# Hyena's transforms folded over mirrored tokens, and its filters' transforms over even and odd times

## The chip, the core and the metric

The kernel runs on one core of a Trainium2 chip. The metric is the device time of one execution in microseconds (us), median of several runs. TensorE is PE in the rows (PEld its weight loads), VectorE DVE, ScalarE ACT, GpSimd POOL, SyncE SP; SP issues the DMAs. All engines run their own instruction streams in the order written and meet only at semaphores.

## The reference, cut to what matters

Two blocks of layers follow each other. The first has two layers on 512 tokens (x) and 256 context tokens (ctx). Of its mixers (attention of 8 heads, a Fourier mix, a Hyena mix) the change touches the Hyena mix and the filters that it convolves with:

```
def hyena_filters(L, w1, b1, freq, w2, b2, w3):
    ...
    h = jnp.sin(freq * (h @ w2 + b2))
    h = (h @ w3).astype(f32)
    ...
    h = h * jnp.tile(decay, (1, 2))
    h_fwd, h_bwd = h[:, :HYENA_W], h[:, HYENA_W:]
    k = jnp.concatenate([h_fwd, jnp.zeros((1, HYENA_W), f32), h_bwd[:0:-1]], axis=0)
    return k / jnp.sum(jnp.abs(k), axis=0, keepdims=True)

def hyena_mix(u, conv_w, conv_b, w1, b1, freq, w2, b2, w3, d_bias):
    u = short_conv(u, conv_w, conv_b)
    x0, x1, v = jnp.split(u, 3, axis=-1)
    z = (x1 * v).astype(jnp.float32)
    k = hyena_filters(L, w1, b1, freq, w2, b2, w3)
    zf = jnp.fft.rfft(z, n=2 * L, axis=1)
    kf = jnp.fft.rfft(k, n=2 * L, axis=0)
    y = jnp.fft.irfft(zf * kf[None], n=2 * L, axis=1)[:, :L] + d_bias.astype(jnp.float32) * z
    return (x0.astype(jnp.float32) * y).astype(u.dtype)
```

HYENA_W is 256 channels. Layer 0 mixes x (L = 512) and ctx (L = 256), layer 1 only x. So there are three filters: two for 512 times (0 and 1), one for 256 (2).

## The kernel before

Stages follow each other with a barrier between them. In the stages that matter here every piece of work is a "thread" that yields due times (plain numbers), and `run_braided` writes each engine's program by merging the threads in order of those times. The numbers only set the order; an engine waits at a semaphore wherever it has to.

**The opening** (`opening`) loads and turns the tokens (`EnterThread`), multiplies the condition vector with a layer's modulation weights (`ModulationThread`, L3068 on PE), and makes the three filters (`FilterThread`). A filter is two small layers with sines, then L3283 on PE, scaled by the decay on DVE (L3335) and formed into sum and difference `pm` (L3337, L3338), the sum of magnitudes (L3289), its reciprocal on DVE, and the transform L3300: per block f of 128 frequencies, 2 parts (cosine, sine) times `nt` tiles of 128 times, each an fp32 product of 128x256 with the table `tk`. DVE scales the result into `kf` (L3350). PSUM bank 7 serves the even blocks of all three filters; the odd ones have a bank per filter. SP stores the filters to memory, and the next stage starts after these stores.

**The mixers** (`mixers`, once a layer) put the attention in units of two 128-token blocks, in pitch W. In a unit u PE does scores(u) (L1688), the turning of the first half of the last unit's probabilities (L1703), values of the unit before that (L1715), the turning of the other half (L1703), and then a fill: a piece of other work. scores(u+1) waits for ACT's second exponential of unit u, and that one waits for the second turning, whose buffer it writes. The fills are the heads' projections (L1570 to L1582) and the Hyena work (`HyenaThread`): `fill(u)` is unit u's place. Layer 0 has 24 units and ctx's Hyena work too, layer 1 has 16 units.

The Hyena thread of one sequence: DVE convolves and multiplies to z (`col(4 + b)`, b = 0, 1, two groups of 128 channels) early in the stage; at fill(0) (ctx: fill(10)) PE turns z (L1844) and ACT keeps it as `zt` (L1878); per block f PE transforms it with the table `ta` (L1857), a bank for both parts, and DVE multiplies with the filter into `yf` (L1915 to L1920); per b PE transforms back with the same table (L1867) and DVE adds d*z and multiplies with x0 (L1926, L1929). In layer 0 the four blocks f of x are at fill(1), (2), (4), (5), the two inverses at fill(7), (8); ctx has both f at fill(11) and both b at fill(13). In layer 1 two blocks f are at fill(1), two at fill(3), the inverses at fill(5) and fill(7). On DVE, unit u's maximum (L1774), reciprocal (L1780) and scaling (L1782) stand at due times 2.6 and 3.6 after the unit's start.

An fp32 matmul of the program is two PE records in the trace; a turning is one.

## Time and profile before

| | |
|---|---|
| runs (us) | 3737.94, 3743.83, 3743.93; median 3743.83 |
| profiled execution | span 3744.0 us; no other time of that execution is given |
| PE busy | 3505.1 us (94%), 17782 records |
| PEld / DVE / ACT / POOL busy | 76% / 53% / 36% / 4% |
| opening, 0 to 135 us | PE busy 106.2, DVE 65.3, ACT 34.3 |
| mixers of layer 0, 268 to 560 us | PE busy 270.0, DVE 147.6, ACT 100.5 |
| mixers of layer 1, 1310 to 1475 us | PE busy 157.0, DVE 83.9, ACT 55.1 |

A matmul's record lasts longer than the distance to the next one, since matmuls are pipelined; what a group of them costs is read from the start of the first to the start of what follows. An idle time in brackets is that of the engine just before the row, with what ended it.

### The profile page before, as it was taken

The numbers are of one execution on the slowest core, as the hardware profiler recorded it, in microseconds if no ns is written. First come the engines' busy times: TensorE is split into PE (matmuls) and PEld (weight loads), VectorE is DVE, ScalarE is ACT, GpSimd is POOL, SyncE is SP. The second block draws the span as 40 slices with busy tenths as digits, with TensorE's granted clock in tenths as the row PEclk, the third lists the DMA queues.
The fourth block names the chain that finished last, engine by engine and source line by source line (L and its number), as shares of the span: only waits on it lengthen the run. The fifth ranks groups of instructions, "written<-read, shape, count | busy, mean of one in ns | idle before, by whom it ended". The sixth has DMA issues, their size and how long they took to land.

```text
span 3744.0 us, 42762 instructions
## 1 busy us (share of the span) xinstructions
PE 3505.1 (94%) x17782; PEld 2844.8 (76%) x17782; DVE 1971.7 (53%) x2697; ACT 1352.1 (36%) x1896; POOL 144.0 (4%) x108
## 2 busy tenths in 40 slices
PE   7899988899999999889998997999889999979998
PEld 2684557788888755688887887888778888778887
DVE  5566446577655454466556665333445455553333
ACT  3322334422323333353345556222433333362223
POOL 0000000000000000000000004000400000040001
PEclk9999999999999999999998998999999999989998
DMA  5442003345444230145532221323233323213231
GB/s 177 129 153 72 12 1 109 111 149 162 152 157 130 79 107 1 46 140 185 192 117 68 68 68 57 98 94 99 59 81 72 87 68 90 67 57 102 90 99 48
DMA packets 366624, 360.65 MB, mean 96 GB/s; under 512 B 65071, under 2 KB 312030, under 8 KB 365023
## 3 DMA queue, kind: packets, MB, share of 16 engines
q1 hardware_dynamic: 366211, 357.84, 31.2%
q8 instruction: 141, 2.31, 0.3%
q14 instruction: 52, 0.43, 0.0%
q10 hardware_dynamic: 220, 0.07, 0.0%
HBM read 350.02 MB, written 4.72 MB: 95 GB/s over the span
## 4 chain that ended last, share of the span: by engine, by line
PE 47%; DVE 5%; ACT 4%; POOL 1%; issue 1%; DMA 0%; SPq 0%; POOLq 0%; DVEq 0%; ACTq 0%
PE ps L403 41%; PE ps L2530 1%; DVE r_st L2424 1%; ACT second_w_hi L490 1%; DVE second_w_lo L549 1%; ACT second_scr L685 1%; PE ps L2551 1%; PE ps L2553 1%; POOL sums L467 1%; PE ps L2303 1%; POOL sq L464 1%; PE ps L2540 1%; DVE x_res L870 0%; DVE second_scr L868 0%; DVE second_scr L696 0%
## 5 line engine op out<-in xcount | busy, mean ns | idle before, releaser
L403 PE MATMUL ps<-second_h_hi,second_w_hi 128*128 128x512 f32 (+1 forms) x2216 | 831.4, 375 | 51.6 <-DVE second_h_lo L896 18.1
L403 PE MATMUL ps<-second_h_hi,second_w_lo 128*128 128x512 f32 (+1 forms) x2216 | 811.8, 366 | 0.0
L403 PE MATMUL ps<-second_h_lo,second_w_hi 128*128 128x512 f32 (+1 forms) x2216 | 811.8, 366 | 0.0
L549 DVE TENSOR_TENSOR second_w_lo<-ring,second_w_hi 128x2048 fp32r<-128x2048 f32 (+2 forms) x176 | 390.5, 2219 | 480.6 <-ACT second_w_hi L490 480.6
L403 PEld LDWEIGHTS ps<-second_h_hi,second_w_hi 128*128 128x128 f32 x2216 | 430.2, 194 | 120.2 <-issue 29.4
L403 PEld LDWEIGHTS ps<-second_h_hi,second_w_lo 128*128 128x128 f32 x2216 | 429.0, 194 | 65.4
L403 PEld LDWEIGHTS ps<-second_h_lo,second_w_hi 128*128 128x128 f32 x2216 | 430.3, 194 | 63.4 <-issue 1.9
L490 ACT ACTIVATE second_w_hi<-ring 128x2048 fp32r<-128x2048 f32 (+2 forms) x176 | 311.4, 1769 | 309.1 <-PE ps L403 301.0
L403 PE MATMUL ps<-h_mix_hi,w_hi 128*128 128x512 f32 (+3 forms) x776 | 272.2, 351 | 24.0 <-DVE h_mix_lo L712 16.5
L403 PE MATMUL ps<-h_mix_lo,w_hi 128*128 128x512 f32 (+3 forms) x776 | 268.7, 346 | 0.0
L403 PE MATMUL ps<-h_mix_hi,w_lo 128*128 128x512 f32 (+3 forms) x776 | 268.0, 345 | 0.0
L403 PEld LDWEIGHTS ps<-h_mix_hi,w_hi 128*128 128x128 f32 (+1 forms) x776 | 148.8, 192 | 45.6 <-issue 11.1
L403 PE MATMUL ps<-hid_hi,w_hi 128*128 128x256 f32 (+1 forms) x512 | 173.5, 339 | 0.0
L403 PE MATMUL ps<-hid_lo,w_hi 128*128 128x256 f32 (+1 forms) x512 | 172.3, 337 | 0.0
L403 PE MATMUL ps<-hid_hi,w_lo 128*128 128x256 f32 (+1 forms) x512 | 172.1, 336 | 0.0
L1072 DVE SCALAR_TENSOR_TENSOR side_a<-side_w,cond,side_a 128x512 f32<-128x512 f32 x224 | 157.2, 746 | 21.7 <-DMA side_w<-in_w_mod 16.8
L490 ACT ACTIVATE w_hi<-ring 128x2048 fp32r<-128x2048 f32 x50 | 95.3, 1905 | 187.4 <-PE ps L403 180.4
L403 PEld LDWEIGHTS ps<-h_mix_lo,w_hi 128*128 128x128 f32 (+1 forms) x776 | 148.7, 192 | 18.1 <-issue 0.8
L403 PEld LDWEIGHTS ps<-h_mix_hi,w_lo 128*128 128x128 f32 (+1 forms) x776 | 148.3, 191 | 18.0
L549 DVE TENSOR_TENSOR w_lo<-ring,w_hi 128x2048 fp32r<-128x2048 f32 x50 | 114.6, 2292 | 80.5 <-ACT w_hi L490 80.5
L403 PE MATMUL ps<-second_hid_hi,second_w_hi 128*128 128x512 f32 (+1 forms) x424 | 152.0, 358 | 0.0
L403 PE MATMUL ps<-second_hid_lo,second_w_hi 128*128 128x512 f32 (+1 forms) x424 | 151.0, 356 | 0.0
(402 smaller groups left out, 5763.9 us busy)
## 6 DMA issues: line engine op xcount, KB each, us to landing
ring<-in_w_mlp SPq DMA_DIRECT2D x64, 1024.0 KB, 5.4
side_w<-in_ada_w SPq DMA_DIRECT2D x96, 512.0 KB, 4.8
ring<-in_ffn_w_in SPq DMA_DIRECT2D x44, 1024.0 KB, 5.1
side_w<-in_w_mod SPq DMA_DIRECT2D x80, 512.0 KB, 3.9
ring<-in_attn_w_in SPq DMA_DIRECT2D x48, 512.0 KB, 5.3
ring<-in_hgrn_w_in SPq DMA_DIRECT2D x32, 512.0 KB, 4.9
ring<-in_ffn_w_out SPq DMA_DIRECT2D x16, 1024.0 KB, 5.0
ring<-in_w_in SPq DMA_DIRECT2D x14, 1024.0 KB, 5.5
```

The source lines that it names most:

```text
L403: mm = pe.matmul(acc, lhsT, rhs, start=k == 0 and wp == ap, stop=k == j.kt - 1 and wp == 1)
L464: pool.tensor_tensor(dst[:, 1, :], y, x, ALU.mult).then_inc(*S["sums_product"].one)
L467: pool.tensor_tensor(acc[:, parts, :], acc[:, parts, :], dst[:, parts, :], ALU.add).then_inc(*S["sums_added"].one)
L490: act.activation(unit.place(unit.slot[0]), unit.place(M.ring[:, u % RING, :]), ACT.Copy).then_inc(*S.w_hi.one)
L549: dve.tensor_tensor(unit.place(unit.slot[1]), unit.place(M.ring[:, u % RING, :]), unit.place(unit.slot[0]), ALU.subtract).then_inc(*S.w_lo ...
L685: f = act.activation(scr[:, k, :], scr[:, k, :], ACT.Identity, scale=self.scale(ks.start + k, a), bias=self.bias(ks.start + k, a))
L1072: p = dve.scalar_tensor_tensor(a, src, col, a, ALU.mult, ALU.add)
L2303: mm = pe.matmul(M.ps[:, 5, c], B.st[:, m, :], B.qs[:, c], start=False, stop=m == self.N_CHUNKS - 1, skip_group_check=True)
L2424: o = dve.scalar_tensor_tensor(B.st[:, m + 1, :], B.st[:, m, :], B.eb[:, m * CHUNK + CHUNK - 1:m * CHUNK + CHUNK], add, ALU.mult, ALU.add)
L2530: mm = pe.matmul(self.y_ps[:, i * P:(i + 1) * P], values, p_t(i)[:, k, :], start=m == 0, stop=m == len(tiles) - 1)
L2540: tr = pe.transpose(self.t_ps[:, k * P:(k + 1) * P], M.f[:, i % 2, k * P:(k + 1) * P], M.ident[:, :])
L2551: pe.matmul(self.s_ps[:, 0:LX], every4(qk[:, 0, :], u), qk[:, 1, :], start=True, stop=True)
```

## The change

**Hyena transforms.** DVE forms, just ahead of fill(0) (fill(10) for ctx), sum and difference of z and mirrored z into the new tile `uv`, and PE turns `uv` in the place of z. A block f then needs one half of the turned tiles for each part: nt/2 products in the place of nt, with the table `ta` of half the size. The inverse makes two half results (for sum and difference) of length/2 columns each, with a table `ti`, and DVE unfolds them: two operations add d*z, two add or subtract the other half, each on half the columns. The two tables of a sequence are two DMAs in the place of one, with the same bytes together; `uv` lies where the Fourier tables and later `yf` lie. **Filters.** The times are sorted into even and odd ones (decay and embedding too). A pair of blocks of frequencies needs one transform of the even and one of the odd times, each nt/2 products a part, and their sum and difference are the two blocks. DVE scales each half into `mag` and then forms sum and difference on 128x512 elements. The table `tk` has half the bytes: 1 MB in the place of 2 MB for 512 times.

```
-        self.ta = sb("mx_ta", [P, self.nt, 2, length], 44)
+        self.half = length // 2
+        self.ta = sb("mx_ta", [P, self.nt // 2, 2, length], 44)
+        self.ti = sb("mx_ti", [P, self.nt, 2, self.half], 52)
+        self.uv = sb("mx_uv", [P, 2, length], 64)
...
-        sp.dma_start(self.ta[:, :, :, :], X.io[f"hy_ta_{self.length}"]).then_inc(*S.landing("hyena_ta_landed").one)
+        landed = S.landing("hyena_tables_landed")
+        sp.dma_start(self.ta[:, :, :, :], X.io[f"hy_ta_{self.length}"]).then_inc(*landed.one)
+        sp.dma_start(self.ti[:, :, :, :], X.io[f"hy_ti_{self.length}"]).then_inc(*landed.one)
...
-                tr = pe.transpose(M.ps[:, bank, t * P:(t + 1) * P], self.col(4 + b)[:, t * P:(t + 1) * P],
-                                  M.ident[:, :])
+                tr = pe.transpose(M.ps[:, bank, t * P:(t + 1) * P], self.uv[:, b, t * P:(t + 1) * P], M.ident[:, :])
...
             for c in range(2):
-                for t in range(nt):
+                folded = (c + self.odd(f)) % 2 * (nt // 2)
+                for t in range(nt // 2):
                     mm = pe.matmul(M.ps[:, bank, c * HY:(c + 1) * HY], self.ta[:, t, c, f * P:(f + 1) * P],
-                                   self.zt[:, t, :], start=t == 0, stop=t == nt - 1)
+                                   self.zt[:, folded + t, :], start=t == 0, stop=t == nt // 2 - 1)
...
-            X.banks.claim(pe, bank, (S["hyena_part"], self.z0 + b + 1))
+            X.banks.claim(pe, bank, (S["hyena_part"], 2 * (self.z0 + b) + 2))
             pe.wait_ge(S["hyena_mixed"].sem, S["hyena_mixed"].at(self.f0 + nt))
-            for f in range(nt):
-                for c in range(2):
-                    mm = pe.matmul(M.ps[:, bank, 0:length], self.yf[:, f, c, b * P:(b + 1) * P], self.ta[:, f, c, :],
-                                   start=f == 0 and c == 0, stop=f == nt - 1 and c == 1)
+            for part in range(2):
+                for f in range(nt):
+                    c = (part + self.odd(f)) % 2
+                    mm = pe.matmul(M.ps[:, bank, part * self.half:(part + 1) * self.half],
+                                   self.yf[:, f, c, b * P:(b + 1) * P], self.ti[:, f, c, :], start=f == 0, stop=f == nt - 1)
...
-                dve.tensor_tensor(self.col(b), self.col(b - 2), self.col(b), ALU.mult).then_inc(*S["hyena_z"].one)
+                dve.tensor_tensor(self.col(b), self.col(b - 2), self.col(b), ALU.mult).then_inc(*S["hyena_product"].one)
+        yield self.t_z - 1.5
+        dve.wait_ge(S["hyena_product"].sem, S["hyena_product"].at(self.z0 + 2))
+        dve.wait_ge(S["fourier_acc"].sem, S["fourier_acc"].at(2 if X.last else 4))
+        if self.before:
+            dve.wait_ge(S["hyena_acc"].sem, S["hyena_acc"].at(self.z0))
+        h, n = self.half, self.length
+        for b in range(2):
+            z = self.col(4 + b)
+            dve.tensor_tensor(self.uv[:, b, 0:h], z[:, 0:h], z[:, n - 1:h - 1:-1], ALU.add)
+            dve.tensor_tensor(self.uv[:, b, h:n], z[:, 0:h], z[:, n - 1:h - 1:-1], ALU.subtract)\
+                .then_inc(*S["hyena_z"].one)
...
-            z, x0 = self.col(4 + b), self.col(b)
-            part = S["hyena_part"]
-            dve.scalar_tensor_tensor(z, z, M.col("hy_d", X.l, b), M.ps[:, 6 + b, 0:self.length], ALU.mult, ALU.add)\
-                .then_inc(*part.one)
-            dve.wait_ge(part.sem, part.at(self.z0 + b + 1))
+            z, x0, h, n = self.col(4 + b), self.col(b), self.half, self.length
+            even, odd = M.ps[:, 6 + b, 0:h], M.ps[:, 6 + b, h:n]
+            part, d = S["hyena_part"], M.col("hy_d", X.l, b)
+            up, down = z[:, 0:h], z[:, n - 1:h - 1:-1]
+            dve.scalar_tensor_tensor(up, up, d, even, ALU.mult, ALU.add)
+            dve.scalar_tensor_tensor(down, down, d, even, ALU.mult, ALU.add).then_inc(*part.one)
+            dve.wait_ge(part.sem, part.at(2 * (self.z0 + b) + 1))
+            dve.tensor_tensor(up, up, odd, ALU.add)
+            dve.tensor_tensor(down, down, odd, ALU.subtract).then_inc(*part.one)
+            dve.wait_ge(part.sem, part.at(2 * (self.z0 + b) + 2))
...
-        self.tk = sb("tk", [P, nt, 2, length])
+        self.tk = sb("tk", [P, nt, 2, length // 2])
...
-            bank = (7, b)[f % 2]
-            X.banks.claim(pe, bank, (made["kf"], f + 1))
+            pair, side = divmod(f, 2)
+            bank = (7, b)[side]
+            X.banks.claim(pe, bank, (made["scaled"], f + 1))
             for c in range(2):
-                for t in range(nt):
-                    mm = pe.matmul(M.ps[:, bank, c * HY:(c + 1) * HY], T_.tk[:, t, c, f * P:(f + 1) * P],
-                                   self.pm[:, t, c, :], start=t == 0, stop=t == nt - 1)
+                times = (c + side) % 2 * (nt // 2)
+                for t in range(nt // 2):
+                    mm = pe.matmul(M.ps[:, bank, c * HY:(c + 1) * HY], T_.tk[:, times + t, c, pair * P:(pair + 1) * P],
+                                   self.pm[:, times + t, c, :], start=t == 0, stop=t == nt // 2 - 1)
...
+            pair, side = divmod(f, 2)
             self.wait(dve, "dft", f + 1)
-            dve.tensor_tensor(self.kf[:, f, :, :], M.ps[:, (7, b)[f % 2], :].rearrange("p (c n) -> p c n", c=2), inv,
-                              ALU.mult).then_inc(*made["kf"].one)
+            dve.tensor_tensor(self.half_sums[side], M.ps[:, (7, b)[side], :].rearrange("p (c n) -> p c n", c=2), inv,
+                              ALU.mult).then_inc(*made["scaled"].one)
+            if side:
+                self.wait(dve, "scaled", f + 1)
+                dve.tensor_tensor(self.kf[:, pair, :, :], self.half_sums[0], self.half_sums[1], ALU.add)
+                dve.tensor_tensor(self.kf[:, nt // 2 + pair, :, :], self.half_sums[0], self.half_sums[1], ALU.subtract)\
+                    .then_inc(*made["kf"].one)
...
-        a = 2 * np.pi * np.outer(i, i + 0.5) / (2 * n)
+        times, lower = np.concatenate([i[0::2], i[1::2]]), i[0::2]
+        a = 2 * np.pi * np.outer(times, lower + 0.5) / (2 * n)
         out[f"hy_tk_{n}"] = by_tile(np.stack([np.cos(a), np.sin(a)], 1))
-        a = 2 * np.pi * np.outer(i + 0.5, i + 0.5) / (2 * n)
-        out[f"hy_ta_{n}"] = by_tile(np.stack([np.cos(a), np.sin(a)], 1))
+        freqs = np.concatenate([lower, n - 1 - lower])
+        a = 2 * np.pi * np.outer(i[:n // 2] + 0.5, freqs + 0.5) / (2 * n)
+        both = np.stack([np.cos(a) + np.sin(a), np.cos(a) - np.sin(a)])
+        out[f"hy_ta_{n}"] = by_tile(both.transpose(1, 0, 2))
+        out[f"hy_ti_{n}"] = by_tile(0.5 * both.transpose(2, 0, 1))
```

What this makes of the engines' programs. First PE in layer 0's mixers where z is turned, before: the row of L1844 is the turning, L1688 ahead of it is scores(0), behind it scores(1).

```order
L1688 MATMUL ps<-mx_k_0_2015,mx_q_0_2013 128x512
L1844 MATMUL ps<-ident,p 128x128 [waits hyena_z,lower_shifted]
L1844 MATMUL ps<-ident,p 128x128 x3
L1844 MATMUL ps<-ident,p 128x128 [waits hyena_z,lower_shifted]
L1844 MATMUL ps<-ident,p 128x128 x3
L1688 MATMUL ps<-mx_k_0_2015,mx_q_0_2013 128x512 [waits exp_ready]
```

And after:

```order
L1688 MATMUL ps<-mx_k_0_1994,mx_q_0_1992 128x512
L1853 MATMUL ps<-ident,mx_uv0x 128x128 [waits hyena_z,lower_shifted]
L1853 MATMUL ps<-ident,mx_uv0x 128x128 x3
L1853 MATMUL ps<-ident,mx_uv0x 128x128 [waits hyena_z,lower_shifted]
L1853 MATMUL ps<-ident,mx_uv0x 128x128 x3
L1688 MATMUL ps<-mx_k_0_1994,mx_q_0_1992 128x512 [waits exp_ready]
```

The place is the same; what is turned is now `uv`, and `hyena_z` is now given by the operations that make it. Those stand on DVE behind both scalings of unit 0 and ahead of unit 1's maxima. Before:

```order
L1774 TENSOR_REDUCE nmax<-ps 128x1 [waits scores_ready] x2
L1780 RECIPROCAL rsum<-esum 128x1 [waits exp_ready]
L1782 TENSOR_SCALAR f<-f,rsum 128x768 [waits reciprocal_ready]
L1780 RECIPROCAL rsum<-esum 128x1 [waits exp_ready]
L1782 TENSOR_SCALAR f<-f,rsum 128x768 [waits reciprocal_ready]
L1774 TENSOR_REDUCE nmax<-ps 128x1 [waits scores_ready] x2
```

And after:

```order
L1780 RECIPROCAL rsum<-esum 128x1 [waits exp_ready]
L1782 TENSOR_SCALAR f<-f,rsum 128x768 [waits reciprocal_ready]
L1918 TENSOR_TENSOR mx_uv0x<-p 128x256 [waits vectors,hyena_product]
L1919 TENSOR_TENSOR mx_uv0x<-p 128x256
L1918 TENSOR_TENSOR mx_uv0x<-p 128x256
L1919 TENSOR_TENSOR mx_uv0x<-p 128x256
L1774 TENSOR_REDUCE nmax<-ps 128x1 [waits scores_ready] x2
```

So four operations came between unit 0's last scaling and unit 1's first maximum. Last, DVE at the end of the opening, before:

```order
L3350 TENSOR_TENSOR flt_filt<-ps,flt_inv 128x512 [waits filter1_dft,filter2_inv]
L3350 TENSOR_TENSOR flt_filt<-ps,flt_inv 128x512 [waits filter2_dft]
L3350 TENSOR_TENSOR flt_filt<-ps,flt_inv 128x512 [waits filter1_dft]
L3350 TENSOR_TENSOR flt_filt<-ps,flt_inv 128x512 [waits filter2_dft]
L3086 TENSOR_TENSOR mods<-ps,vec 128x32 [waits modulation_turned]
```

And after:

```order
L3380 TENSOR_TENSOR flt_mag<-ps,flt_inv 128x512 [waits filter1_dft,filter2_inv]
L3380 TENSOR_TENSOR flt_mag<-ps,flt_inv 128x512 [waits filter2_dft]
L3380 TENSOR_TENSOR flt_mag<-ps,flt_inv 128x512 [waits filter1_dft]
L3384 TENSOR_TENSOR flt_filt<-flt_mag 128x512 [waits filter1_scaled]
L3385 TENSOR_TENSOR flt_filt<-flt_mag 128x512
L3380 TENSOR_TENSOR flt_mag<-ps,flt_inv 128x512 [waits filter2_dft]
L3384 TENSOR_TENSOR flt_filt<-flt_mag 128x512 [waits filter2_scaled]
L3385 TENSOR_TENSOR flt_filt<-flt_mag 128x512
L3112 TENSOR_TENSOR mods<-ps,vec 128x32 [waits modulation_turned]
```

Each pair of blocks brings two operations more, and the last pair's stand ahead of the modulation's last step.

## Rows read from the trace of the kernel before

**Rows 1.** Groups by shape on PE: layer 0's mixers, layer 1's, and the opening

```profile
L1857 PE MATMUL ps<-mx_zt0x,mx_ta0x 128*128 128x256 f32 x64 | 14.5, 379 | 0.0
L1867 PE MATMUL ps<-mx_ta0x,mx_yf0x 128*128 128x512 f32 x32 | 14.1, 592 | 0.0
L1857 PE MATMUL ps<-mx_zt0c,mx_ta0c 128*128 128x256 f32 x16 | 3.6, 379 | 0.0
L1867 PE MATMUL ps<-mx_ta0c,mx_yf0c 128*128 128x256 f32 x16 | 3.6, 379 | 0.0
...
L1857 PE MATMUL ps<-mx_zt1x,mx_ta1x 128*128 128x256 f32 x64 | 14.1, 379 | 0.0
L1867 PE MATMUL ps<-mx_ta1x,mx_yf1x 128*128 128x512 f32 x32 | 14.1, 592 | 0.0
...
L3300 PE MATMUL ps<-flt_pm,tk 128*128 128x256 f32 x144 | 33.1, 384 | 1.9 <-DVE flt_filt L3350 1.9
```

**Rows 2.** Timeline of PE, fills of layer 0 and what follows (start, us)

```profile
359.34 3.62 PE L1857 MATMUL ps<-mx_zt0x,mx_ta0x 128*128 128x256 f32 x16
362.80 2.75 PE L1688 MATMUL ps<-mx_k,mx_q 96*128 96x512 f32 x8
...
410.26 7.03 PE L1867 MATMUL ps<-mx_ta0x,mx_yf0x 128*128 128x512 f32 x16
417.13 1.03 PE L1688 MATMUL ps<-mx_k,mx_q 96*128 96x256 f32 x4
```

**Rows 3.** Timeline of PE, a unit of layer 0 with no fill

```profile
501.42 0.84 PE L1703 MATMUL ps<-ident,f 128*128 128x128 f32 x6
503.59 1.13 PE L1688 MATMUL ps<-mx_k,mx_q 96*128 96x256 f32 x4 [1.32 <-ACT f L1749]
```

**Rows 4.** Timeline of PE and DVE, layer 0 at fill(0)

```profile
338.71 1.04 PE L1844 MATMUL ps<-ident,p 128*128 128x128 f32 x8
342.69 5.49 PE L1688 MATMUL ps<-mx_k,mx_q 96*128 96x512 f32 x8 [2.95 <-ACT f L1749]
...
342.87 0.62 DVE L1782 TENSOR_SCALAR f<-f,rsum 128x768 f32<-128x768 f32 x1
```

**Rows 5.** Timeline of PE, layer 1 at fill(0)

```profile
1363.26 1.04 PE L1844 MATMUL ps<-ident,p 128*128 128x128 f32 x8
1367.24 2.85 PE L1688 MATMUL ps<-mx_k,mx_q 96*128 96x512 f32 x8 [2.95 <-ACT f L1749]
```

**Rows 6.** Timeline of PE and DVE, ctx's turning at fill(10) of layer 0

```profile
447.00 0.60 PE L1844 MATMUL ps<-ident,p 128*128 128x128 f32 x4
448.49 1.13 PE L1688 MATMUL ps<-mx_k,mx_q 96*128 96x256 f32 x4 [0.89 <-ACT f L1749]
...
448.84 0.62 DVE L1782 TENSOR_SCALAR f<-f,rsum 128x768 f32<-128x768 f32 x1
```

**Rows 7.** Timeline of DVE, two operations of 128x256 in a row

```profile
62.26 0.42 DVE L3337 TENSOR_TENSOR flt_pm<-flt_filt 128x256 f32<-128x256 f32 x1
62.60 0.42 DVE L3338 TENSOR_TENSOR flt_pm<-flt_filt 128x256 f32<-128x256 f32 x1
```

**Rows 8.** Stretches around both fills(0): busy us of each engine, then PEclk (granted clock)

```profile
343.00:348.00 5.00, 5.00 (x9) 2.47 (x9) 0.49 (x1) 0.62 (x2) 0.00 (x0) 0.50 0.85 290
1361.00:1368.00 7.00, 4.05 (x18) 2.56 (x17) 3.35 (x6) 2.74 (x7) 0.00 (x0) 1.00 0.00 0
```

**Rows 9.** Timeline of DVE, end of the opening and start of the next stage

```profile
131.20 0.69 DVE L3350 TENSOR_TENSOR flt_filt<-ps,flt_inv 128x512 f32<-128x512 f32 x1 [4.76 <-PE ps L3300]
...
134.99 1.23 DVE L696 TENSOR_TENSOR f<-x_res,rs 128x1024 f32<-128x1024 f32 x1 [2.73 <-PEq L166]
```

**Rows 10.** Timeline of PE early in the opening; then a DMA issue, KB, us to landing

```profile
30.43 1.23 PE L3175 MATMUL ps<-ident,f 128*128 128x128 f32 x8 [2.23 <-DMA f<-in_x]
...
40.63 5.29 PE L3068 MATMUL ps<-wm,cond 128*2 128x512 f32 x8 [1.96 <-ACT rows L3052]
...
tk<-in_hy_tk SPq DMA_DIRECT2D x1, 2048.0 KB, 13.7
```

More of the change, by code:

```diff
@@ L1822, in col, with odd @@
         return self.X.M.p[:, 8 + b, self.lo:self.lo + self.length]
+    def odd(self, f):
+        return f // (self.nt // 2)
     def sync(self, sp):
@@ L1850, in tensor @@
             if f == 0:
-                landed = S.landing("hyena_ta_landed")
-                pe.wait_ge(landed.sem, landed.at(2 if self.before else 1))
+                landed = S.landing("hyena_tables_landed")
+                pe.wait_ge(landed.sem, landed.at(4 if self.before else 2))
                 pe.wait_ge(S["hyena_zt"].sem, S["hyena_zt"].at(self.z0 + 2))
@@ L1918, in vector @@
             chain(dve, step, dve.tensor_tensor(m[:, 1, :], zc, k1, ALU.mult))
-            dve.tensor_tensor(y0, y0, m[:, 0, :], ALU.add)
-            dve.tensor_tensor(y1, y1, m[:, 1, :], ALU.subtract).then_inc(*S["hyena_mixed"].one)
+            dve.tensor_tensor(y0, y0, m[:, 0, :], ALU.subtract)
+            dve.tensor_tensor(y1, y1, m[:, 1, :], ALU.add).then_inc(*S["hyena_mixed"].one)
         for b in range(2):
@@ L3237, in __init__ @@
         self.kf = self.filt[:, :, :].rearrange("p t (c n) -> p t c n", c=2)
+        self.half_sums = [self.mag[:, i, :].rearrange("p (c n) -> p c n", c=2) for i in range(2)]
         S = X.S
         self.made = {k: S[f"filter{i}_{k}"] for k in ("pe", "ang", "red", "sin", "filt", "abs", "sum", "half", "inv",
-                                                       "dft", "kf")}
+                                                       "dft", "scaled", "kf")}
     def t_f(self, f):
@@ L3259, in sync @@
         yield self.t_f(self.tables.nt) + 4
-        self.wait(sp, "kf", T_.nt)
+        self.wait(sp, "kf", T_.nt // 2)
         sp.dma_start(X.M.filters[self.l, T_.length], self.kf).then_inc(*S.landing("filters_stored").one)
@@ L3456, in tables @@
         ang = ang.astype(np.float32).astype(f)
-        out[f"hy_emb_{n}"] = np.concatenate([tt, np.cos(ang), -np.sin(ang)], -1).T
+        out[f"hy_emb_{n}"] = np.concatenate([tt, np.cos(ang), -np.sin(ang)], -1)[times].T
         dec = np.exp(-tt * deltas)
@@ L3461, in tables @@
         both[0, HY:] = 0.0
-        out[f"hy_decay_{n}"] = by_tile(both)
+        out[f"hy_decay_{n}"] = by_tile(both[times])
     out["chunk_resets"] = np.broadcast_to((t % CHUNK != 0).astype(f), (P, LX))
```

## The prediction

> **What bounds the kernel now.** I read four views. First the groups by shape, which give what the change touches: PE's transforms are 14.5, 14.1, 3.6 and 3.6 us of busy time in layer 0, 14.1 and 14.1 us in layer 1, and 33.1 us in the opening [rows 1]. Busy time counts each record with its overlap, so I take costs from the timeline, start to start: 16 records of 256 columns took 362.80 - 359.34 = 3.46 us, 0.216 each, and 16 records of 512 columns 417.13 - 410.26 = 6.87 us [rows 2]. In both places the row behind a fill starts with no idle time in brackets, so PE runs from one to the next and the fill lies on the path.
>
> Then I asked what would be late if the fill were shorter. In a unit without one, PE ended its second turning (start 501.42) and had to wait for ACT's exponential until 503.59; 1.32 us of that is idle [rows 3]. So a fill shorter than about 1.4 us is free, and one of 1.7 us or more still costs all that lies above. The halved fills stay above it: 1.73 us for a block of x, and more for the rest. What is taken from them should come off the span in full.
>
> Third, the timeline at fill(0), which the change loads with a new dependency. PE turned z at 338.71, stood idle for 2.95 us and began scores(1) at 342.69 when ACT's second exponential was there; DVE's last scaling of unit 0 started at 342.87 [rows 4]. Layer 1 has the same 2.95 us [rows 5], ctx's turning in layer 0 0.89 us [rows 6]. Last, the granted clock around both fills(0) [rows 8] and the two ends of the opening [rows 9, 10].
>
> **The change part by part.** The execution profiled has a span of 3744.0 us, 0.2 above the median of the runs; nothing is known of time outside the span, so I subtract from 3744.0 and leave the rest.
>
> Filters on PE: 144 records become 72, so 72 x 0.216 = 15.6 us go [rows 1, 2]. In the second half of the opening PE's program is nearly gapless (its L3300 waits for DVE sum to 1.9 us [rows 1]); with shorter blocks DVE's scaling follows closer and I give back 0.3. Remains 15.3. Bounds: 15.6, and 9 if the reciprocals and the bank shared by the three filters, whose waits are now covered by products, surface at every filter.
>
> Filters on DVE: five pairs of blocks get two operations of 128x512 each, ten in all. They lie beside PE's work except the last pair's, which stand between the last scaling and the modulation's last step, the store, and the barrier. A 128x512 operation took 0.69 us there [rows 9], so +1.4. The next stage starts 134.99 - 131.20 = 3.8 us after that scaling starts in both kernels. Bounds 1.2 to 1.4.
>
> Filter tables: `tk` has 1 MB less. It took 13.7 us to land, ahead of tokens for which PE then stood idle for 2.23 us [rows 10]. 2048 KB in 13.7 us is a rate that takes over 5 us for 1 MB, shared with other transfers; that reaches to cover the gap. The next wait in the chain, for ACT, is 1.96 us [rows 10] and could swallow it. Bounds 0 to 2.2 saved; I take 1.8, since ACT's work there itself follows PE's turnings.
>
> Opening together: 15.3 - 1.4 + 1.8 = 15.7 us.
>
> Hyena, forward: x's four blocks in layer 0 have 64 records, 32 go: 6.9 us. Layer 1 the same, 6.9 us. ctx: 8 of 16 go: 1.7 us, and its fill of 1.73 us stays above the 1.4 [rows 1 to 3].
>
> Hyena, inverse: as many records as before with half the columns. 16 records of 256 columns in the place of 512: 6.87 - 3.46 = 3.4 us for each b, 6.8 us a layer, 13.6 together [rows 2]. ctx goes from 256 to 128 columns; no fp32 product of that size stands in my rows. Half of 0.216 would save 1.7 us; if a weight load sets the pace, nothing. I take 1.7 (the other sizes scale with columns) and keep 0.
>
> PE's sum in the mixers: layer 0: 6.9 + 6.8 + 1.7 + 1.7 = 17.1; layer 1: 6.9 + 6.8 = 13.7.
>
> The new wait at fill(0): DVE's four operations start after the scaling of 342.87, at about 343.45. Two of 128x256 in a row start 0.34 us apart and last 0.42 [rows 7]. The second is done at 344.2, the fourth at 344.9. PE turns the first group at 344.3, the second from 344.95; four turnings are about half of a set of eight that took up to 1.04 us [rows 4], so scores(1), queued behind them, starts at 345.45 in the place of 342.69: +2.8 us. All softmax work of unit 1 is behind scores(1), so nothing hides it. Layer 1 is the same picture: +2.8. For ctx the last scaling starts at 448.84, and scores(11) was at 448.49 [rows 6]. 128 columns stand in no row; between the 0.34 of 256 columns and nothing I take 0.2 an operation. Four of them from 449.4, the last one's tail of 0.3 and the second turning of 0.3 end at 450.6: +2.1 us (bounds 1.3 and 2.7). Together +7.7. The mirrored operand is read backwards, which no row shows. If it doubled an operation, the twelve would add 8 x 0.34 + 4 x 0.2 = 3.5 us; if it is free, as I take it, 0.
>
> DVE's longer unfolding: per b one operation of 512 columns becomes four of 256, some 4 x 0.34 - 0.7 = +0.7 us more [rows 7, 9], beside PE's fill or head projections of the unit; the scaling behind it is needed only in the next unit. Cost 0; if that cover were gone, 0.7 in each of six places, 4.2. The tables of a sequence are two DMAs with the same bytes, needed some 70 us later: 0.
>
> The clock: in layer 0 the 2.95 us gap ended with the granted clock at 0.50 (1.2 GHz) from 343 to 348, and eight records of scores(1) took 5.3 us; in layer 1 after the same gap the clock stayed at 1.00 (2.4 GHz) and they took 2.7 [rows 4, 5, 8]. The gap grows to 5.6 us in layer 0 and 4.7 us in layer 1. Layer 0 pays already; layer 1 will probably pay 5.3 - 2.7 = 2.6 us, at three in four 2.0. Bounds 0 to 8 (both layers and ctx longer).
>
> The Trainium skill (TensorE: Matmul & The Clock Gate, section "Why this matters for your kernels") warns of idle gaps between bursts of matmuls, after which the array drops to 1.2 GHz. That speaks against the change at these places; layer 0's rows agree with it, layer 1's do not at 2.95 us. Taken as certain, the rule makes it 2.6 in the place of 2.0, 3707.8 us; taken for more places it is rival (a).
>
> Sum: 15.7 + 17.1 + 13.7 - 7.7 - 2.0 = 36.8 us. 3744.0 - 36.8 = 3707.2 us.
>
> **The rivals.** (a) The clock turns against it in more places: a thinner PE program in the attention leaves more idle time, and each cold stretch costs as in layer 0, 2.6 us on one scores group and as much again on what follows. For it: a gap of 2.95 us once sufficed. Against it: halved fills leave no new gap beyond the 1.32 us of a bare unit, and behind that gap four records of 256 columns took 1.13 us in all, no more than behind a fill (1.03) but for a tenth [rows 2, 3]. Two or three such stretches, and backward reading at a price: 8 to 14 us less gain, 3715 to 3721.
>
> (b) The opening keeps its length: something else than PE sets its end, the stores or the chain of reciprocals. Against it: DVE waited 4.76 us for PE's last block [rows 9]. Then 12 to 15 us less: about 3720.
>
> (c) ACT takes PE's place in the mixers, so that shorter fills turn into waits. Were the exponential 1.7 us later than the bare unit shows, each of the twelve shortened fills would lose that, 20 us: 3728. Or, with (b), no measurable change. [rows 3] speaks against it.
>
> (d) Slower: the clock gate does more than single stretches. If the thinned attention made the array run at 1.2 GHz over whole units, each us of PE work there would cost one more. The gain of 36.8 us is gone once 37 us of what PE then does run cold; a quarter of the 390 us of PE busy time left in both mixers would be 97 us, 3744 + 60 = 3804. Against it: the bare unit is the thinnest there is now, and its records took what those behind a fill took [rows 2, 3].
>
> (e) More than forecast: the tokens' earlier landing passes in full, the cold stretch in layer 0 vanishes by a better phase, and layer 1 stays warm: 3707.2 - 0.4 - 2.6 - 2.0 = 3702.2, and somewhat less with runs as low as the lowest.
>
> That the change does not do what it says is out: the order of the changed kernel has half the products for each block.
>
> **How the numbers follow.** Forecast 0.68 (3702 to 3714), (a) 0.12, (b) 0.05, (c) 0.04, (d) 0.03, (e) up to 3702 0.08. The range 3697 to 3721 holds the first, (a), half of (b) and most of (e), with the spread of the runs, 6 us. What a measurement can tell from no change is 0.2%, 7.5 us: faster means below 3736.3. Faster 0.94: all of the forecast, (a), (b), (e) and a little of (c); same 0.03; slower 0.03, (d).
>
> **What would show it.** The next stage's first DVE operation near 119 in the place of 134.99. Fills of x at 1.7 us forward and 3.4 us inverse, with no idle time before the scores behind them. At both fills(0) PE's turning starts some 5 us after scores(0) has ended, and waits for DVE's `uv`; scores(1) right behind it. PEclk 0.50 after it in both layers. It would be wrong if the scores after fills show brackets with ACT, if the opening ends after 125, or if the stretch behind 1475 us has another length than before.

## The result and the profile after

The changed kernel took 3712.35 us (median; 3709.2 to 3713.33), the kernel before 3740.91 us in the same comparison: ratio 0.9917 [0.9905, 0.9929]. In a second comparison it was 3707.59 against 3744.82 us, 0.9900 [0.9887, 0.9914]. The forecast was 3707.2 us, 36.8 us under the span of before. The two comparisons give a gain of 28.6 and 37.2 us.

First the page of the changed kernel: span, then busy time of PE and its records. Before there were 3505.1 us and 17782 records.

```profile
span 3707.4 us, 42520 instructions
PE 3458.4 (93%) x17638; PEld 2817.5 (76%) x17638; DVE 1985.4 (54%) x2737; ACT 1352.7 (36%) x1896; POOL 144.6 (4%) x108
```

PE has 46.7 us less work; 36.6 of them left the span. The groups by shape (busy us, mean ns of one, idle time before) answer to [rows 1]: layer 0, layer 1, opening.

```profile
L1866 PE MATMUL ps<-mx_zt0x,mx_ta0x 128*128 128x256 f32 x32 | 7.6, 379 | 0.0
L1877 PE MATMUL ps<-mx_ti0x,mx_yf0x 128*128 128x256 f32 x32 | 7.2, 379 | 0.0
...
L1877 PE MATMUL ps<-mx_ti0c,mx_yf0c 128*128 128x128 f32 x16 | 1.9, 275 | 0.0
L1853 PE MATMUL ps<-ident,mx_uv0x 128*128 128x128 f32 x8 | 1.9, 424 | 5.4 <-DVE mx_uv0x L1919 5.4
...
L1853 PE MATMUL ps<-ident,mx_uv1x 128*128 128x128 f32 x8 | 1.9, 421 | 5.4 <-DVE mx_uv1x L1919 5.4
...
L3329 PE MATMUL ps<-flt_pm,tk 128*128 128x256 f32 x72 | 18.9, 412 | 3.1 <-DVE flt_mag L3380 3.1
```

The transforms are about half of what they were. Those of Hyena have no idle time in front of them; those of the filters wait 3.1 us for DVE, where they waited 1.9 [rows 1]. On PE's timeline a forward fill, then an inverse, each with what follows, answer to [rows 2]:

```profile
336.22 1.89 PE L1866 MATMUL ps<-mx_zt0x,mx_ta0x 128*128 128x256 f32 x8
337.95 1.03 PE L1688 MATMUL ps<-mx_k,mx_q 96*128 96x256 f32 x4
...
1395.42 3.62 PE L1877 MATMUL ps<-mx_ti1x,mx_yf1x 128*128 128x256 f32 x16
1398.87 2.74 PE L1688 MATMUL ps<-mx_k,mx_q 96*128 96x512 f32 x8
```

1.73 us for 3.46, and 3.45 for 6.87. What is new is idle time that ends with DVE: in front of the `uv` turnings and in the opening. The timeline of PE and DVE at fill(0) of layer 0 (start, us) answers to [rows 4]:

```profile
319.77 2.74 PE L1688 MATMUL ps<-mx_k,mx_q 96*128 96x512 f32 x8
327.95 1.94 PE L1853 MATMUL ps<-ident,mx_uv0x 128*128 128x128 f32 x8 [5.44 <-DVE mx_uv0x L1919]
329.68 4.21 PE L1688 MATMUL ps<-mx_k,mx_q 96*128 96x512 f32 x8
...
327.05 0.42 DVE L1918 TENSOR_TENSOR mx_uv0x<-p 128x256 f32<-128x256 f32 x1
327.38 0.42 DVE L1919 TENSOR_TENSOR mx_uv0x<-p 128x256 f32<-128x256 f32 x1
327.71 0.42 DVE L1918 TENSOR_TENSOR mx_uv0x<-p 128x256 f32<-128x256 f32 x1
328.05 0.42 DVE L1919 TENSOR_TENSOR mx_uv0x<-p 128x256 f32<-128x256 f32 x1
```

scores(1) start 9.91 us after scores(0), 6.56 before: +3.35. Mirrored operands are read at the pace of others, 0.34 us apart. The turning took 1.94 us for 1.04: it ran at half clock as well. Next the end of the opening, PE and DVE, which answers to [rows 9]:

```profile
106.29 1.10 PE L3329 MATMUL ps<-flt_pm,tk 128*128 128x256 f32 x4 [2.18 <-DVE flt_mag L3380]
107.32 0.58 PE L3103 MATMUL ps<-ident,rows 2*128 2x2 f32 x4
107.84 3.42 PE L3329 MATMUL ps<-flt_pm,tk 128*128 128x256 f32 x8
...
103.66 1.75 DVE L3373 RECIPROCAL flt_inv<-flt_inv 128x256 f32<-128x256 f32 x1
...
120.99 1.22 DVE L696 TENSOR_TENSOR f<-x_res,rs 128x1024 f32<-128x1024 f32 x1 [2.71 <-PEq L166]
```

The opening is 14.0 us shorter. The scaling that PE waits 2.18 us for stands right behind the context filter's reciprocal on DVE, and the block that follows takes 3.42 us for the 1.9 to 2.0 of its neighbours. Last the three places where PE now waits longer behind DVE's unfolding of the inverses: in layer 0 through the head's rope, which is queued behind it, and in layer 1 once through the bank that the unfolding reads and once through the rope. The last line is from the kernel before, which waited at the second of them already:

```profile
412.15 1.05 PE L1578 MATMUL ps<-p,mx_wkv 128*64 128x256 f32 x4 [0.92 <-DVE mx_q L1620]
...
1406.98 2.84 PE L1570 MATMUL ps<-p,mx_wq 128*128 128x512 f32 x6 [1.17 <-DVE p L1953]
...
1434.48 1.05 PE L1578 MATMUL ps<-p,mx_wkv 128*64 128x256 f32 x4 [0.29 <-DVE mx_q L1620]
...
1438.77 2.84 PE L1570 MATMUL ps<-p,mx_wq 128*128 128x512 f32 x6 [0.25 <-DVE p L1926]
```

### The profile page after: what moved, and what is told of

The parts are those of the page before. It is cut to its first block, busy times and chain, and to the rows that moved or that the text cites. A ratio compares the mean times of both kernels' runs of the same rounds, so it can differ in the third digit from the quotient of the medians.

```text
span 3707.4 us, 42520 instructions
## 1 busy us (share of the span) xinstructions
PE 3458.4 (93%) x17638; PEld 2817.5 (76%) x17638; DVE 1985.4 (54%) x2737; ACT 1352.7 (36%) x1896; POOL 144.6 (4%) x108
## 4 chain that ended last, share of the span: by engine, by line
PE 47%; DVE 5%; ACT 4%; POOL 1%; issue 1%; DMA 0%; SPq 0%; POOLq 0%; DVEq 0%; ACTq 0%
PE ps L403 42%; PE ps L2556 1%; DVE r_st L2450 1%; ACT second_w_hi L490 1%; DVE second_w_lo L549 1%; ACT second_scr L685 1%; PE ps L2577 1%; PE ps L2579 1%; POOL sums L467 1%; PE ps L2329 1%; POOL sq L464 1%; PE ps L2566 1%; DVE x_res L870 0%; DVE second_scr L868 0%; DVE second_scr L696 0%
```

## The experiments

Medians against the kernel before in the same comparison:

| kernel | us | ratio, 95% |
|---|---|---|
| changed, again (`r_after`) | 3707.59 | 0.9900 [0.9887, 0.9914] |
| `filters_only` | 3733.52 | 0.9965 [0.9953, 0.9977] |
| `hyena_only` | 3723.54 | 0.9944 [0.9932, 0.9957] |
| `uv_early` | 3702.68 | 0.9889 [0.9875, 0.9902] |
| `pe_kept_busy` | 3706.94 | 0.9903 [0.9889, 0.9918] |
| `unfold_early` | 3709.92 | 0.9909 [0.9894, 0.9924] |
| `sum_early` | 3708.71 | 0.9908 [0.9893, 0.9923] |
| `uv_early_busy` | 3698.79 | 0.9883 [0.9867, 0.9900] |
| before, again (`before_again`) | 3741.93 | 0.9997 [0.9988, 1.0006] |
| `tk_full` | 3711.41 | 0.9915 [0.9902, 0.9929] |
| `three_moves` | 3696.60 | 0.9873 [0.9858, 0.9888] |
| `all_with_busy` | 3695.99 | 0.9874 [0.9861, 0.9888] |

Each interval is some 10 us wide, so the small terms are read from the profiles, place by place: the distance between two instructions on either side of the edit. How little a span says of a small term shows in what no edit touches: from the last scores of layer 1's mixers to the end, the fourteen profiles took between 2209.6 and 2216.7 us, the two of the kernel before 2216.5 and 2211.2.

**The changed kernel again.** No edit.

> The changed kernel again, to see how much of the difference between the two profiles (span 3707.4 against 3744.0, 36.6 us) and the difference between the two medians (28.6 us) is the same thing. Theory A (the first profiled execution of the changed kernel was a fast one, the gain is that of the medians): median 3710 to 3714, span of the new profile 3709 to 3712, and its 2 to 4 us more than 3707.4 are spread over stretches that the change does not touch, above all those where PE runs at half clock. Theory B (the profile before was a slow execution): median as under A, span again 3707 to 3708. In both, the head's end of layer 0 and of layer 1 attention keep their lengths within 0.5 us.

Median and span, 3707.59 and 3704.7, are both below what either theory gave. The changed kernel's median moved by 4.8 us down between the comparisons, that of before by 3.9 us up: 28.6 us was no better a figure than 36.6. The waits are the same to 0.01 us (5.43, 2.84, 5.44); scores(1) take 3.96 and 3.89 us, 4.21 and 4.14 in the first profile.

**The filters alone, the Hyena transforms alone.** The first has the old `HyenaThread` and its table, the second the old filter loop:

```
-                for t in range(nt // 2):
-                    mm = pe.matmul(..., T_.tk[:, times + t, c, pair * P:(pair + 1) * P], ...)
+                for t in range(nt):
+                    mm = pe.matmul(..., T_.tk[:, t, c, f * P:(f + 1) * P], ...)
```

> The new filters' transforms alone (32 and 8 block products halved, the 1 MB table), with the Hyena transforms of before (it uses the new order of the filters' frequencies in its element-wise product, so that product pairs other frequencies than the reference does; the work is the same). Theory: the gain of the opening stands by itself, 14.0 us as the traces show at the first instruction behind the opening, time 3727 (3725 to 3729), and no stall is added in either attention stage. Rival (the opening would have waited for the modulation weights anyway): 3739 to 3741. If the 8 us by which the medians gained less than the profiles lie in the opening, 3733.

> The new Hyena transforms alone (sums and differences, 256-wide tables), with the filters' transforms of before; their table only has its columns in the new order. Theory: layer 0's attention gains 13.1 us and layer 1's 7.7 us as the offsets of the two traces say, 20.8 us together, time 3720 (3718 to 3723), with the waits of 5.44 us for the sums at the first fill of both layers and 2.84 us in the context's. Rival (the gain is that of the medians less the opening's 14.0): 14.6 us, time 3726. With filters_only it says whether the two halves add up: sum of both gains 34.8 under the theory, 28.6 under the rival.

Gains of the medians 11.3 and 21.3 us, 32.6 together, between the 28.6 and 37.2 of the whole: each half gains, and they add up within the scatter (in the same comparison the whole gave 37.2). In the profile `filters_only` starts the next stage at 121.70 us, 13.3 before [rows 9]; `hyena_only` at 133.22, and it shows the 5.43 us wait again. The 3733 of `filters_only`, which its text foresaw only for a loss in the opening, did not come from there. In its profile the span is 11.2 us shorter than before and the opening 13.3; of the 2.1 us between them 1.7 lie around scores(1), which were at half clock in both layers. Its runs lie between 3726.8 and 3736.8; for those without a profile the source stays open.

```profile
329.05 4.54 PE L1688 MATMUL ps<-mx_k,mx_q 96*128 96x512 f32 x8 [2.95 <-ACT f L1749]
...
1354.30 5.49 PE L1688 MATMUL ps<-mx_k,mx_q 96*128 96x512 f32 x8 [2.94 <-ACT f L1749]
```

**The sums earlier.**

```
-        self.uv = sb("mx_uv", [P, 2, length], 64)
+        self.uv = sb("mx_uv", [P, 2, length], 60)
...
-        yield self.t_z - 1.5
+        yield self.t_z - 7.7
...
-        dve.wait_ge(S["fourier_acc"].sem, S["fourier_acc"].at(2 if X.last else 4))
...
-            dve.wait_ge(S["hyena_acc"].sem, S["hyena_acc"].at(self.z0))
+            dve.wait_ge(S["hyena_f"].sem, S["hyena_f"].at(self.f0))
...
-            act.wait_ge(S["hyena_turned"].sem, S["hyena_turned"].at(self.z0 + b + 1))
+            if b == 0:
+                act.wait_ge(S["hyena_turned"].sem, S["hyena_turned"].at(self.z0 + 2))
```

> The changed kernel with the sums and differences formed about 6 us earlier, in the place that the turned tokens take later (free since the Fourier tables don't reach it), so that PE finds them ready when it comes to turn them; the copies out of PSUM then wait for both turnings. Theory (the wait for DVE's subtraction at the three first fills is what the forecast paid 7.7 us for, 3.35 + 2.16 + 3.35 = 8.9 us in the trace, and the cold blocks behind the two long ones are its consequence, 1.0 us of turning and 1.3 us of scores each): idle before the turning 2.1 us in both x fills instead of 5.44 (what was there before the change, 2.95, less nothing), time 8.9 to 13.5 us under r_after, 3699 to 3704. Rival 1 (the idle time belongs to the exponentials and not to the subtraction): no gain, 3710 to 3714. Rival 2 (the sums now delay the first row maxima on DVE): 2 to 4 us gained less, 3702 to 3707.

PE at both fills(0) of this kernel:

```profile
323.81 1.04 PE L1853 MATMUL ps<-ident,mx_uv0x 128*128 128x128 f32 x8
327.79 4.54 PE L1688 MATMUL ps<-mx_k,mx_q 96*128 96x512 f32 x8 [2.95 <-ACT f L1749]
...
1332.12 1.04 PE L1853 MATMUL ps<-ident,mx_uv1x 128*128 128x128 f32 x8
1336.11 5.49 PE L1688 MATMUL ps<-mx_k,mx_q 96*128 96x512 f32 x8 [2.94 <-ACT f L1749]
```

The wait for DVE is gone and the 2.95 us of before is back, as the forecast's step had it (the 2.1 us in the text was a slip of mine). From scores(0) to the first fill it saves 2.8 us in layer 0 and 1.6 in layer 1 against the second profile of the changed kernel, and 2.1 at the context's turning: 6.4 in the profiles, 4.9 in the medians. The profiles' gain is under 8.9 because scores(1) got colder: 4.54 and 5.49 us for 3.96 and 3.89. So part of what the wait had cost is now paid as half clock. From scores(0) to scores(1) it takes 6.56 us again, so the earlier sums delay no row maxima (rival 2 of the text).

**PE kept busy.** 44 (context: 20) of these ahead of the wait; `uv_early_busy` is `uv_early` with 22 at each token fill:

```
+                for _ in range(44 if length == LX else 20):
+                    pe.transpose(M.ps[:, bank, 0:P], M.ident[:, :], M.ident[:, :])
```

> The changed kernel with transposes of the identity on PE ahead of the turning of the sums, 44 of them before the token fills and 20 before the context's, whose results nobody reads; they fill the 5.44 us and 2.84 us in which PE waits for DVE's subtraction. Theory (the idle time costs twice: once itself, and once because the turning and the scores behind it then run at half clock, 1.94 us for 0.97 and 3.9 to 4.2 us for 2.85): the wait's length stays, the turning falls to 1.0 us and scores(1) to 2.85 us, 2.0 to 2.3 us less in each layer, time 4 to 4.6 us under the changed kernel's 3707.6: 3703. Rival (the clock falls for other reasons than the idle time): durations as before, 3707 to 3709. If the transposes take longer than the wait, the difference comes on top; 44 at 0.12 us are 5.3 us.

> uv_early with 22 transposes of the identity ahead of the turning in both token fills. In uv_early PE waited 2.95 us for the exponentials behind the turning, and scores(1) then took 4.54 and 5.49 us at half clock for 2.85. Theory (same mechanism as pe_kept_busy): no idle time over 0.5 us in front of scores(1), which take 2.85 us, so 1.7 and 2.6 us less than uv_early, 4.3 us together; against the changed kernel about 10 us, 3697 to 3699. Rival (the clock falls from something other than the wait): as uv_early, 3702.

The first at layer 0, then the second:

```profile
323.59 4.97 PE L1853 MATMUL ps<-ident 128*128 128x128 f32 x44
329.10 1.39 PE L1856 MATMUL ps<-ident,mx_uv0x 128*128 128x128 f32 x8 [0.54 <-DVE mx_uv0x L1922]
330.32 2.75 PE L1688 MATMUL ps<-mx_k,mx_q 96*128 96x512 f32 x8
```

```profile
326.01 1.04 PE L1856 MATMUL ps<-ident,mx_uv0x 128*128 128x128 f32 x8
327.59 2.85 PE L1688 MATMUL ps<-mx_k,mx_q 96*128 96x512 f32 x8 [0.54 <-ACT f L1749]
```

The stretches of the first with the 44 transposes, and with what follows, have a granted clock of 1.00 (the column behind the engines' busy times):

```profile
323.00:329.00 6.00, 5.56 (x46) 4.87 (x44) 4.01 (x9) 1.88 (x4) 0.00 (x0) 1.00 1.00 366
329.00:333.00 4.00, 3.79 (x17) 2.48 (x18) 0.71 (x3) 1.20 (x2) 0.00 (x0) 1.00 0.64 200
```

With work in the gap scores(1) run at full clock in all four places. They do in the two of `all_with_busy` too. Without the transposes 19 of 22 such places were at half clock (counted below). So the idle time is what lowers the clock here, though 2.95 us of it does not always do so. (The Trainium skill, TensorE: Matmul & The Clock Gate, section "Part 4: PE-mode transpose", says that transposes don't count as busy in the same way and don't bring the full clock. Here they at least kept it for 5 us.) From scores(0) to the first fill `pe_kept_busy` takes 14.4 us in layer 0 and 14.5 in layer 1 where the changed kernel's second profile has 16.2 in both: 1.8 and 1.7 us. Its median is only 0.7 us lower, inside the scatter, where 4 to 4.6 us were expected. `uv_early_busy` is 3.9 us under `uv_early`; at the two places its profile has 1.7 and 2.8 us less.

**The unfolding earlier.**

```
-            yield self.t_b[b] + 7 * self.length / LX
+            yield self.t_b[b] + (3.5 if b == 1 or X.last else 7) * self.length / LX
```

> The changed kernel with DVE's five unfolding instructions of the second inverse in layer 0, and of both in layer 1, due 3.5 us after the inverse is (the inverse now takes 3.5 us) instead of 7 us, ahead of the row maxima of the unit that follows. Theory (the forecast took the unfolding as hidden; the trace shows PE waiting 0.92 us for the roped query, 1.17 us for the unfolding itself and 0.29 us again, all because DVE starts the unfolding only when the next head's rope is due): these three waits go, row maxima start no later (0.4 us to spare), 2.4 us less, 3705. Rival (DVE has more work now, so a wait only moves: the maxima start late and the exponentials and the turning with them): 3707 to 3709, with idle time behind ACT's exponentials longer by what the waits lost.

PE in front of the rope and of the next head, layer 1 (before the edit 1.17 us idle there):

```profile
1406.79 0.87 PE L1703 MATMUL ps<-ident,f 128*128 128x128 f32 x6
1407.50 2.74 PE L1570 MATMUL ps<-p,mx_wq 128*128 128x512 f32 x6
```

The three waits are gone. From the scores behind an inverse to the next scores it takes 1.10, 1.4 and 0.5 us less, 3.0 together, with nothing longer behind; `three_moves` repeats it (1.1, 1.4 and 0.5 against `uv_early`). Not all of this had been lost by the change: against the kernel before, the changed kernel is longer at these places by 0.91 (13.77 for 12.86), 0.92 (13.60 for 12.68) and 0.48 us (12.65 for 12.17), 2.3 together. The median shows nothing (3709.9, runs 3704.7 to 3712.4). The profile is of the fastest of these runs, and even there the context's 2.84 us wait was followed by half clock, which costs 2.9 us and did not happen in the two profiles of the changed kernel. What made the other runs longer stays open.

**The magnitude sums earlier.**

```
-        yield self.start + 27
+        yield self.start + (26 if self.i == 2 else 27)
```

> The changed kernel with the context filter's magnitude sums (two products on PE) ahead of the last-but-one block of modulation weights, not behind it. Theory (filter 2's reciprocal now ends the opening: PE waits 2.18 us for its first scaled block at 106.3 us and then runs a block at half clock, 3.42 us for 1.9): the wait and the cold block go, 3 to 3.7 us less, 3704. Rival (the opening ends with the last modulation weights, whatever PE does before): the idle time moves to the modulation product in front of the end, no gain, 3707 to 3708.

```profile
104.93 1.10 PE L3329 MATMUL ps<-flt_pm,tk 128*128 128x256 f32 x4 [0.94 <-DVE flt_mag L3380]
105.97 0.40 PE L3103 MATMUL ps<-ident,rows 2*128 2x2 f32 x4
106.30 1.99 PE L3329 MATMUL ps<-flt_pm,tk 128*128 128x256 f32 x8
...
118.02 1.23 DVE L696 TENSOR_TENSOR f<-x_res,rs 128x1024 f32<-128x1024 f32 x1 [2.71 <-PEq L166]
```

The wait falls by 1.24, the cold block by 1.43 us, and the opening ends 3.0 us earlier (117.85 in `three_moves`), so the last modulation weights were not its limit. The median, 3708.7 where 3704 was expected, again hides it, with the same cold stretch in the context's unit:

```profile
421.85 1.08 PE L1853 MATMUL ps<-ident,mx_uv0c 128*128 128x128 f32 x4 [2.84 <-DVE mx_uv0c L1919]
422.73 1.91 PE L1688 MATMUL ps<-mx_k,mx_q 96*128 96x256 f32 x4
424.43 1.49 PE L1703 MATMUL ps<-ident,f 128*128 128x128 f32 x6
425.85 3.76 PE L1715 MATMUL ps<-mx_probs,mx_v 128*64 128x256 f32 x12
```

From the turning to the next fill this took 8.40 us, and 5.71 in the changed kernel's first profile: 2.7 us for the same instructions behind the same wait.

**The kernel before again, and the full table.** `tk_full` declares `tk` with `length` columns in the place of `length // 2`.

> The kernel before once more, for a second profile. Theory (what differs between two executions of one kernel is which short stretches of PE run at half clock): span 3738 to 3745, waits of the same length at the same places, and layer 1's scores(1), 2.85 us at full clock in the first profile, may take up to 5.5 us; in the kernel with new filters alone the same instructions took 5.49 us. If so, the 2.0 us that the forecast set down for the change as its share of the clock in layer 1 is the difference between two states that either kernel can be in, not a cost of the change. Rival (the order of events ahead of it decides, always the same in one kernel): 2.85 us again.

> The changed kernel with the filters' table at its former size (2 MB, its columns twice, PE reads the first half). Theory (the smaller table lets the input's tokens land earlier; forecast 1.8 us): the first turning of tokens starts at 30.4 us, not at 27.8 to 28.5, PE waits 2.2 us for the DMA there, and the opening ends 1.9 us later; 3709.5. Rival (the tokens wait for other transfers): start at 28 us, no change in time, 3707 to 3708; the profile decides, the time is within the scatter.

scores(1) of both layers in the second profile of before, to be read against [rows 4, 5]:

```profile
338.70 2.85 PE L1688 MATMUL ps<-mx_k,mx_q 96*128 96x512 f32 x8 [2.94 <-ACT f L1749]
...
1361.80 5.49 PE L1688 MATMUL ps<-mx_k,mx_q 96*128 96x512 f32 x8 [2.94 <-ACT f L1749]
```

The picture is turned round: layer 0 warm, layer 1 cold. In `tk_full` the tokens' turning starts at 29.66 us behind 1.88 us of idle time, at 28.53 and 27.77 in the changed kernel, and the next stage starts at 122.83, not at 120.99 and 121.25. So the smaller table is worth 1.1 to 1.9 us where it lands, 1.6 to 1.8 at the end. The other profiles agree: in the four with the 2 MB table the turning starts at 29.6 to 30.4 us, in the ten with 1 MB at 27.5 to 28.5.

**Together.** `three_moves` is `uv_early`, `unfold_early` and `sum_early` in one; `all_with_busy` adds the 22 transposes.

> uv_early, unfold_early and sum_early together, no added work. Theory (each removes its own wait, at places that don't touch): 2.8 + 3.0 + 2.5 us in the sums (what uv_early's profile showed at scores(1) of layer 0, in the context's and in layer 1, part of it given back to half clock), 2.4 us in the unfolding, 3.0 us in the opening, 13.7 us together less up to 3 us for colder scores(1): 3694 to 3697. Rival (the context's 2.84 us wait went cold in unfold_early and sum_early, so that the gains are exchanged for half clock elsewhere): 3700 or more.

> The same three moves with the 22 transposes of the identity in front of the token turnings. Theory: 1.7 to 2.6 us less in each layer than three_moves, as uv_early_busy showed against uv_early (1.9 and 2.8 us at those places), 3690 to 3692, the fastest of all; waits in front of scores(1) 0.54 us. Rival (PE's clock is granted out of a budget, so that the added transposes cost clock elsewhere): no faster than three_moves, with more stretches at half clock behind.

3696.6 and 3696.0 us, each over 1.2% below before. `three_moves` is the version to keep: 10 to 11 us below the changed kernel, with no added work, and in the range that its theory gave. The transposes bring 0.6 us on top, which is nothing that can be told apart, where 1.7 to 2.6 were expected in each layer. In its profile `three_moves` had scores(1) cold in layer 0 (5.49 us) and warm in layer 1 (2.85 us), so only one place was left to mend. There `all_with_busy` takes 3.3 us less from scores(0) to the first fill, but it starts scores(0) 3.1 us later (321.38 for 318.26): 1.1 us of this is there at the end of the opening, 0.8 comes from the first product of layer 0's Fourier stage (6.71 us for 5.91). The rival of its text, a budget of clock, foresaw just this time. Against it, the whole execution of `pe_kept_busy` had a granted clock of 0.971, the changed kernel's 0.969 and 0.968, so there the transposes cost no clock elsewhere. In `all_with_busy` it was 0.969, in `three_moves` 0.970, one profile each; why the gain is lost there stays open.

## Why the forecast was right

**Opening: 15.7 forecast, 12.9 measured.** The seven profiles with new filters and small table whose opening was not edited start the next stage between 120.4 and 121.7 us; the three with the old filters at 134.99, 133.55 and 133.22; the means are 121.0 and 133.9. The step that was mis-sized is "I give back 0.3" in the filters on PE: the L3380 waits have 3.1 us against 1.9, and one block ran cold for 1.4, 2.6 us together. The bound of 9 named the mechanism, reciprocals that surface; `sum_early` shows it for one of three filters and takes 3.0 us back. DVE's tail (1.4 forecast; 5.11 us for 3.79 from the last scaling to the next stage) and the table (1.8; 1.6 to 1.8 in `tk_full`) were right.

**The transforms: 17.1 and 13.7.** A block of x took 337.95 - 336.22 = 1.73 us, an inverse 1398.87 - 1395.42 = 3.45, the context's inverse with 128 columns half of what 256 took (16 records in 1.79 us). This term was right, and by the right way: [rows 3]'s 1.32 us said from where on a shorter fill is free, and none went under it. Rivals (c) and (d) find nothing: no fill has ACT behind it.

**The wait for the sums: 2.8, 2.8 and 2.1 forecast; 3.35, 3.35 and 2.16 measured.** The mechanism is the one given. What is missing, 0.55 us a layer, is the turning, taken at full clock and run at half: `pe_kept_busy`, with the same sums and the clock full, has scores(1) 9.31 us after scores(0), 2.75 over the 6.56 of before. `uv_early` removes the wait. (The forecast's gap of 4.7 us for layer 1 is a slip: by its own working the two layers are alike, and they have 5.44 and 5.44.)

**The unfolding: 0 forecast, 2.3 measured.** The step "needed only in the next unit" failed. It looked at the scaling behind the unfolding and not at the head's rope (L1618 to L1623), queued on DVE behind both, for which PE waits before L1578, nor at the bank that the next head claims. `unfold_early` takes it back in full, and 0.7 us that the kernel before lost already.

**The clock: 2.0 forecast for layer 1.** The number came from one profile that had layer 0 cold and layer 1 warm. Over all profiles, scores(1) behind the 2.95 us gap (before twice, `filters_only`, `uv_early`, `three_moves`: ten places) were cold in seven, 4.54 or 5.49 us, and warm in three; behind the 5.44 us gap (changed kernel twice, `hyena_only`, `unfold_early`, `sum_early`, `tk_full`: twelve places) in all twelve, 3.5 to 4.6 us. The means are 4.51 and 4.02 us; behind the longer gap the turning, already counted in the 3.35, ran at half clock too. From scores(0) to the first fill, which takes in the turning, scores(1) and what is still cold behind them, the ten places took 11.7 to 15.0 us, 13.6 on average, and the twelve 15.9 to 16.9, 16.3 on average: 2.7 us a layer. So beside the wait the clock cost nothing there; it gave 0.7 us a layer back. Rival (a) had its place: the context's new 2.84 us wait was followed by half clock in four of six profiles (the changed kernel's two were spared), for 1.6 us in `hyena_only` and 2.7 to 2.9 us in the others, 1.7 on average, which is not in the sum.

The terms so corrected (opening, transforms of both layers, sums, unfolding, clock in the layers, clock in the context) give 12.9 + 17.1 + 13.7 - 8.9 - 2.3 + 1.4 - 1.7 = 32.2 us; the two comparisons gave 28.6 and 37.2 us, the two halves of the change 32.6 together. So the forecast of 36.8 lies on the high side, and that it is not farther off is in part luck: four terms (opening 2.8, sums 1.2, unfolding 2.3, context's clock 1.7) were 8.0 us too good together, and the clock in the layers 3.4 us too bad. The runs of one kernel, 2 to 11 us apart, cover the rest. Of the signs it named one did not come: the next stage starts at 121.0 us, not near 119. And the length behind the mixers is no sign at all, since it differs by 5.3 us between the two profiles of the kernel before.

## What to carry over

A shorter instruction on the bound engine pays in full as long as it stays longer than the wait it covers; read that wait from a unit of the same loop in which nothing stands there. When work on the second engine grows, ask not who needs its result, but who is queued behind it there and who waits for those: the losses here were of that kind, and each was cured by an earlier place in the order, not by less work. A clock state seen once is not a property of the place: look at a second profile before it becomes a term.

## What the runs showed of the hardware

- A gap of 2.95 us of idle PE, with the same instructions on either side of it, was followed by full clock in three cases and by half clock in seven; the same kernel showed both. In its second profile the kernel before has the clock at full (2.4 GHz) in layer 0, where [rows 8] have 0.50 (1.2 GHz), and half the clock in layer 1, where they have 1.00:

```profile
338.00:343.00 5.00, 3.50 (x14) 2.16 (x14) 2.82 (x5) 2.38 (x5) 0.00 (x0) 1.00 1.01 324
1362.00:1367.00 5.00, 5.00 (x8) 2.55 (x9) 0.59 (x1) 0.72 (x2) 0.00 (x0) 0.50 0.00 0
```

- Transposes whose result nobody reads held the clock: 44 took 4.97 us, 0.11 us apart, and scores(1) behind them 2.75 us where they took 3.5 to 4.6.
- fp32 products of 128 columns cost half of those of 256: 1.79 us for 16 records and 3.46, 0.11 and 0.216 us each.
- A DVE operand with step -1 in the free dimension cost nothing: 128x256 in 0.42 us, 0.34 apart [rows 7].
